# Prompt attention of an MLA decoder step: probabilities transposed on VectorE in 32-by-32 blocks, values taken in 32-row tiles

## What is computed

```python
N_HEADS, QK_NOPE, QK_ROPE, V_HEAD, KV_LORA, SEQ = 16, 64, 32, 64, 256, 1024
def mla_attend_prompt(q_nope, q_rope, c_kv, k_r, w_a_uk, w_a_uv):
    k_nope = jnp.einsum('bsc,chd->bshd', c_kv, w_a_uk)
    v = jnp.einsum('bsc,chd->bshd', c_kv, w_a_uv)
    def block(args):                      # 128 queries at a time
        qn_b, qr_b, i = args
        sc = (jnp.einsum('bqhd,bkhd->bhqk', qn_b, k_nope)
              + jnp.einsum('bqhd,bkd->bhqk', qr_b, k_r)).astype(jnp.float32) * ATTN_SCALE
        sc = jnp.where(k_pos[None, :] <= q_pos[:, None], sc, -jnp.inf)
        p = jax.nn.softmax(sc, axis=-1).astype(v.dtype)
        return jnp.einsum('bhqk,bkhd->bqhd', p, v)
```

## Time and profile before

| | |
|---|---|
| median of 3 runs | 1532.52 us (1532.19 to 1536.1) |
| the profiled execution's own time | 1532.18 us |
| its span, first to last instruction | 1530.5 us |
| PE busy (share of the span) | 1505.8 us (98%) |
| PE weight loads | 1372.2 us (90%) |
| DVE, ACT, POOL busy | 934.7, 551.6, 243.8 us |
| granted PE clock | 0.999 of full |
| DMA | 117.73 MB, mean 77 GB/s |

### The profile page before, as it was taken

The page is one execution under the profiler, slowest core; times in us unless marked ns, Lnnn a source line. Parts: engine busy times, 40 slices in busy tenths (PEclk is TensorE's granted clock), DMA queues, the critical chain, the costliest instruction groups (busy, mean ns, idle before and its releaser), DMA issues.

```text
span 1530.5 us, 32080 instructions
## 1 busy us (share of the span) xinstructions
PE 1505.8 (98%) x11757; PEld 1372.2 (90%) x11757; DVE 934.7 (61%) x1722; ACT 551.6 (36%) x1187; POOL 243.8 (16%) x431
## 2 busy tenths in 40 slices
PE   8999999999999999999999999999999999999998
PEld 7988888888887677778899999999999999999996
DVE  5675667666667788367664645554544545554557
ACT  5465665556664223232331312212131312112146
POOL 2010011101115541000030211212020311112000
PEclk9999999999999999999999999999999999999999
DMA  7112121111133998351220202022020202021003
GB/s 231 51 40 56 38 41 30 39 38 37 23 105 93 301 309 274 112 169 42 81 86 28 69 14 69 15 67 68 20 62 27 69 14 69 14 69 55 1 28 125
DMA packets 158655, 117.73 MB, mean 77 GB/s; under 512 B 55263, under 2 KB 145821, under 8 KB 158416
## 3 DMA queue, kind: packets, MB, share of 16 engines
q1 hardware_dynamic: 143280, 94.40, 20.9%
q10 hardware_dynamic: 11664, 11.44, 2.3%
q0 software_dynamic: 3600, 10.43, 2.1%
HBM read 106.08 MB, written 14.34 MB: 79 GB/s over the span
## 4 chain that ended last, share of the span: by engine, by line
PE 49%; DVE 1%; issue 0%; ACT 0%; DVEq 0%
PE banks L2120 16%; PE banks L2121 16%; PE banks L2122 16%; PE banks L2203 0%; PE banks L2205 0%; PE banks L2204 0%; PE banks L2190 0%; DVEq L1939 0%; DVE weight_stage L2523 0%; DVE down_stage L2523 0%; DVE weight_stage L2536 0%; DVE down_stage L2536 0%; DVE f_stats L2495 0%; ACT up_hi L2345 0%; ACT up_hi L2341 0%
## 5 line engine op out<-in xcount | busy, mean ns | idle before, releaser
L2120 PE MATMUL banks<-act_hi,up_hi 128*128 128x352 f32 (+2 forms) x1040 | 335.5, 323 | 0.8 <-PEq L1691 0.8
L2122 PE MATMUL banks<-act_hi,up_lo 128*128 128x352 f32 (+2 forms) x1040 | 335.4, 323 | 0.0
L2121 PE MATMUL banks<-act_lo,up_hi 128*128 128x352 f32 (+2 forms) x1040 | 335.1, 322 | 0.0
L2120 PEld LDWEIGHTS banks<-act_hi,up_hi 128*128 128x128 f32 x1040 | 195.3, 188 | 1.0 <-issue 1.0
L2121 PEld LDWEIGHTS banks<-act_lo,up_hi 128*128 128x128 f32 x1040 | 195.5, 188 | 0.0
L2122 PEld LDWEIGHTS banks<-act_hi,up_lo 128*128 128x128 f32 x1040 | 195.4, 188 | 0.0
L2423 DVE TENSOR_TENSOR o_t<-o_t,banks 128x352 f32<-128x352 f32 x240 | 121.0, 520 | 95.1 <-PE banks L2122 94.9
L2402 DVE SCALAR_TENSOR_TENSOR conv_out<-conv_in,conv_now,conv_out 128x1072 f32<-128x1072 f32 x42 | 64.7, 1540 | 185.2 <-ACT conv_out L2276 185.2
L1118 DVE TENSOR_REDUCE neg_max<-banks 128x1 f32<-128x896 f32 (+7 forms) x128 | 96.6, 755 | 105.5 <-PE banks L880 104.6
L2267 ACT ACTIVATE conv_in<-banks 128x352 f32<-128x352 f32 x84 | 36.4, 459 | 336.4 <-PE banks L2122 336.4
L2120 PE MATMUL banks<-gated_hi,down_hi 128*128 128x352 f32 x480 | 155.9, 325 | 0.0
(11 more groups left out here) (342 smaller groups left out, 3066.7 us busy)
## 6 DMA issues: line engine op xcount, KB each, us to landing
weight_stage<-in_w_f_up SPq DMA_DIRECT2D x44, 512.0 KB, 4.6
page_slot<-in_cache_kv_latent SPq DMA_DIRECT2D x100, 128.0 KB, 3.7
down_stage<-in_w_f_down SPq DMA_DIRECT2D x22, 512.0 KB, 4.3
page_slot<-in_cache_kv_latent ACTq DMA_DIRECT2D x51, 128.0 KB, 3.8
rope_rows<-in_cache_k_rope SPq DMA_DIRECT2D x256, 16.0 KB, 2.0
rope_slot<-rope_rows SPq DMA_DIRECT2D x16, 256.0 KB, 4.1
z<-in_x_prompt SPq DMA_DIRECT2D x8, 512.0 KB, 3.4
o_blocks<-o_t POOLq DMA_DIRECT2D x30, 128.0 KB, 2.2
```

The source lines that it names most:

```text
L2120: nc.tensor.matmul(o, ws[0], xs[0], start=first, stop=False)
L2121: nc.tensor.matmul(o, ws[0], xs[1], start=False, stop=False)
L2122: return nc.tensor.matmul(o, ws[1], xs[0], start=False, stop=last)
```

## The change

- The probabilities are transposed by DVE in 32-by-32 blocks, SBUF to SBUF, one instruction a unit (`probs_t`); PE's transposes and the copies out of banks 4 and 5 on ACT and DVE go.
- After such a transpose, partitions 32i to 32i+31 hold the keys of a 32-key block for the queries 32i to 32i+31 of the tile. So V must be in all four groups of 32 partitions. DVE transposes it blockwise out of PSUM (`v_t`), SP stores it in DRAM (`store_v`, four DMAs of 1024 pieces of 32 numbers) and loads it back four times per head (`load_v`).
- `values` runs once per head, when its eight units are done: for each of 32 blocks of 32 keys, for each of two sides (four query tiles each), for each of the four groups one matmul with a 32-row, 64-column stationary and 32 to 128 moving columns; side c writes partitions 64c and up, group i writes bank 4+i. That is 240 matmuls per head.
- The units go head by head, query tiles 7, 0, 6, 1, 5, 2, 4, 3.
- The sums of a head stay in one tile; DVE takes one reciprocal per head, and PE makes rows of them with eight small products, the inverse sums broadcast to 64 columns as stationary and the identity as moving operand (`inverse_rows`). The product with the inverse sums is one DVE instruction of 512 columns per head.
- The low halves of q and of the next pair's weights move from DVE to POOL (`q_low`, `split_first`, `split_second`). k's high and low halves are made head by head.
- All stores of the output move from POOL to SP, two DMAs per head. The rope copies are issued by fours (one register load instruction for four pages), 40 per pair in pairs 0 to 5. The first page loads of `decode` move from the first pair to the end.
- `values` of a pair's second head runs in the next pair's step 2, that of the first head in step 10.

```diff
-OWN_AT = {0: "t0", 2: "t1", 3: "ql"}
-NEXT_AT = {4: "wt", 5: "v0", 6: "v1", 8: "k1", 9: "q02", 10: "q12", 11: "q01", 12: "q11", 14: "k0", 15: "q00", 16: "q10"}
-INV_AT = {7: 3, 10: 2, 13: 1}
-SPLIT_AT = {2: "q", 3: "v", 6: "k"}
-VALUES_AT = {5: (3, 0, 2), 7: (3, 2, 4), 9: (2, 0, 2), 11: (2, 2, 4), 14: (1, 0, 4)}
-OUT_AT = {9: 3, 13: 2, 16: 1}
+UNITS = [(hh, t) for hh in range(2) for t in (7, 0, 6, 1, 5, 2, 4, 3)]
+OWN_AT = {0: ["q12", "q11"], 3: ["ql"], 4: ["q10"]}
+NEXT_AT = {5: ["wt"], 6: ["q02"], 7: ["q01"], 8: ["q00"], 11: ["k1"], 12: ["k0"], 13: ["v0"], 14: ["v1"]}
+INV_AT = {1: 1, 9: 0}
+VALUES_AT = {2: 1, 10: 0}
+OUT_AT = {3: 1, 11: 0}
+SIDES = [(0, 2, 5, 7), (6, 4, 3, 1)]
+FIRST_BLOCK, STRIDE = [72, 0], [24, 28]
...
         @block.sync
+            def store_v(p):
+                sp.wait_ge(pj_dve, dve_count(p, "v1"))
+                for a in range(4):
+                    sp.dma_start(m.v_rows[p % 2, a // 2, :, :, 32 * (a % 2):32 * (a % 2) + 32],
+                                 vq[32 * a:32 * a + 32, :, :].rearrange("k a (j d) -> k (a j) d", d=32)).then_inc(v_out, 16)
+            def load_v(p, hh):
+                for i in range(4):
+                    sp.dma_start(v_blocks(p, hh)[32 * i:32 * i + 32, :], m.v_rows[p % 2, hh].rearrange("k j d -> k (j d)")).then_inc(v_in[hh], 16)
+            for p in range(PAIRS - 1):
+                if p:
+                    sp.wait_ge(pv, head(p - 1, 1))
+                    load_v(p, 1)
+                    store_o(p - 1, 1)
+                gather(10 * p + 1, 10 * p + 4)
+                if p + 2 < PAIRS:
+                    sp.wait_ge(w.lo_ok, w.lo_count(p + 1, "q1"))
+                    sp.wait_ge(pj, pj_count(p + 1, "wt"))
+                    w.load(sp, io, p + 2)
+                gather(10 * p + 4, 10 * p + 8)
+                store_o(p, 0)
+                gather(10 * p + 8, 10 * p + 11)
+                store_v(p + 1)
+                v_stored(sp, p + 1)
+                if p + 2 < PAIRS:
+                    load_v(p + 1, 0)
...
         @block.gpsimd
+            for p in range(PAIRS - 1):
+                pool.wait_ge(pj, pj_count(p, "v1"))
+                w.split_first(nc, pool, p + 1)
                 if p:
+                    q_low(p, "q12")
+                    q_low(p, "q11")
+                    q_low(p, "q10")
+                    pool.wait_ge(pj, pj_count(p, "q10"))
+                w.split_second(nc, pool, p + 1)
+                for name in ("q02", "q01", "q00"):
+                    q_low(p + 1, name)
...
         @block.tensor
-            def transposes(p, n):
...
+            def values(p, hh):
+                pe.wait_ge(xt_ok, p * NU + 8 * hh + 8)
+                pe.wait_ge(v_in[hh], (WD_IN if hh == 0 else 0) + 64 * (p + 1))
...
+                for j in range(4 * TT - 4):
+                    for c in range(2):
+                        if slots_at(c, j) is None:
+                            continue
+                        a, b = slots_at(c, j)
+                        blocks = slice(block_of(c, a, j), block_of(c, b - 1, j) + 1, STRIDE[c])
+                        for i in range(4):
+                            r = slice(32 * i, 32 * i + 32)
+                            last = nc.tensor.matmul(ps[64 * c:64 * c + 64, 4 + i, 32 * a:32 * b], v[r, j, :], x[r, hh, blocks, :],
+                                                    start=j == 0, stop=j == last_block(c))
                 last.then_inc(pv, 1)
+            def inverse_rows(p, hh):
...
+                for slot in range(4):
+                    for c in range(2):
+                        last = nc.tensor.matmul(ps[64 * c:64 * c + 64, bank, slot * P:(slot + 1) * P],
+                                                   rinv[:, hh, slot, c:c + 1].to_broadcast([P, V_HEAD]), m.ident[:, :], start=True, stop=True)
...
         @block.vector
+            def v_t(p, name):
+                dve.wait_ge(pj, pj_count(p, name))
+                if p:
+                    dve.wait_ge(v_out, WD_IN + 64 * p)
+                nc.vector.transpose(vq[:, int(name[1]), :], ps[:, proj_bank(p, name), :]).then_inc(pj_dve, 1)
+            def probs_t(p, n):
+                hh, t = UNITS[n]
+                c, slot = side_of(t)
                 dve.wait_ge(pr, p * NU + n + 1)
+                if n % 8 == 0 and p:
+                    dve.wait_ge(pv, head(p - 1, hh))
+                a, wd = block_of(c, slot, 0), (t + 1) * P
+                out = x[:, hh, a:a + wd // 32, :].rearrange("p j c -> p (j c)")
+                nc.vector.transpose(out, prob[n % 2][:, 0:wd]).then_inc(xt_ok, 1)
```

More of the change, by code:

```diff
@@ L578, in load, with swap, split_hi @@
                          [:, :, p * P:(p + 1) * P]).then_inc(self.staged, 16)
[L580 to L588, removed]
+    def swap(self, nc, hh):
+        half, q, rope = ROPE // 2, self.q_staged, (NOPE, 0)[hh]
+        for at, to in ((rope + half, rope + ROPE), (rope, rope + ROPE + half)):
+            last = nc.gpsimd.tensor_copy(q[:, :, hh, to:to + half], q[:, :, hh, at:at + half])
+        return last
+    def split_hi(self, nc, pool):
+        pool.wait_ge(self.staged, self.LOADS)
+        q = self.q_staged
+        self.swap(nc, 0)
+        self.swap(nc, 1).then_inc(self.swapped, 1)
+        pool.wait_ge(self.swapped, 1)
         nc.gpsimd.tensor_copy(self.q_halves[0][:, :, :, :], q[:, :, :, :])
@@ new lines, in load_v, with gather @@
+            def load_v(p, hh):
+                for i in range(4):
+                    sp.dma_start(v_blocks(p, hh)[32 * i:32 * i + 32, :], m.v_rows[p % 2, hh].rearrange("k j d -> k (j d)")).then_inc(v_in[hh], 16)
+            def gather(first, end):
+                for at in range(4 * first, min(4 * end, DEC_BATCH * N_PAGES), 4):
+                    f, b = at // 8, at % 8 // 4
+                    pages = nc.values_load_multi_w_load_instructions(m.pages[0:1, at:at + 4], [sp.engine])[1]
+                    for j, page in enumerate(pages):
+                        sp.dma_start(m.rope_rows[f // 2, :, f % 2, b, j, :],
+                                     io["cache_k_rope"][bass.ds(page, 1)].rearrange("o p c -> (o p) c")).then_inc(gathered, 16)
@@ L747, in _ @@
             sp_pages(nc, io, m, sp, 4)
+            sp.wait_ge(pv, head(PAIRS - 1, 0))
+            load_v(PAIRS - 1, 1)
             sp_pages(nc, io, m, sp, 5)
-            for g in (1, 0):
-                sp.wait_ge(of_ok, seq(PAIRS - 1, g) + 1)
-                o_out(sp, PAIRS - 1, g).then_inc(m.o_last, 16)
+            store_o(PAIRS - 1, 0)
+            store_o(PAIRS - 1, 1)
         @block.gpsimd
@@ L792, in _ @@
             queries(nc, m, 0)
-            for g in (3, 2):
-                store_o(PAIRS - 1, g)
+            pool.wait_ge(pv, head(PAIRS - 1, 0))
+            pool_pages(nc, io, m, pool, 5)
         @block.tensor
@@ L895, in values @@
-            def values(p, g, first, end):
-                at = tp_before(NU - 4 * g)
-                pe.wait_ge(pt_act, p * HALF_TPU + (at + 1) // 2)
-                pe.wait_ge(pt_dve, p * HALF_TPU + at // 2)
-                if first == 0:
-                    pe.wait_ge(pj_act, act_count(p, "t1"))
-                    if seq(p, g):
-                        pe.wait_ge(of_ok, seq(p, g))
-                n = 2 * g + 2
-                for j in range(n * first // 4, n * end // 4):
-                    q = slice(P if j == 2 * g + 1 else 0, 2 * P)
-                    for hh in range(2):
-                        d = slice(hh * V_HEAD, (hh + 1) * V_HEAD)
-                        last = nc.tensor.matmul(ps[d, 6, q], v[:, j, d], pt[:, g % 2, hh, j, q], start=j == 0, stop=j == 2 * g + 1)
-                if end < 4:
-                    return
-                last.then_inc(pv, 1)
@@ L1451, in _ @@
             k = 0
+            for i in range(2):
+                pool.wait_ge(m.o_st[i], 32 * PAIRS)
             for q in range(1, DPAIRS):
```

593 lines of the change are left out of this document (293 added, 300 removed).

## The result

| | before | after |
|---|---|---|
| median of 4 runs | 1533.5 us (1532.2 to 1536.1) | 1686.5 us (1684.6 to 1689.9) |
| ratio | | 1.0998, 95% interval 1.0973 to 1.1022 |
| span, granted PE clock | 1530.5 us, 0.999 | 1684.0 us, 0.942 |

What follows compares the result with a forecast made beforehand. PE was taken to bound the prompt's attention. Pairs 1 to 6 win 33.6 us, pair 0 and the last 6.2, the end loses 3.5: net 36.3 off 1532.2, so 1496 us, range 1476 to 1556.

Steps and rivals of the forecast that it cites:

- What bounds the kernel now: Prompt's attention: PE, busy 98% of the span, sets the pace, 49.1 us a pair.
- What leaves PE, 19.4 us a pair: PE, per pair: transposes of probabilities, V and inverse rows, the old values and changes back to fp32r products go, 19.4 us.
- the inverse rows: PE, per pair: eight small matmuls per head that make rows of inverse sums come on, 2.2 us.
- the values are the open price: PE's new value products, 240 matmuls a head: between 4.1 and 13.6 us, taken as 5.0 a head, 10.0 a pair.
- the lower end: Value products priced by columns alone, as 144 records of 256 columns: 4.1 us a head.
- 0.5 us for narrow rounds: Value products: in half of the 32 key blocks weight loading outlasts 32 moving columns, 0.5 us a head.
- 10.0 of values, 33.3 - 3.0 of DVE, and 3.2 of semaphores: Length of a pair: values and DVE's work mostly not side by side, plus waits, 43.5 us.
- the sum of PE: PE's work per pair after removals and additions: 49.1 - 19.4 + 2.2 + 10.0 = 41.9 us.
- DVE's sum of 33.3: DVE's work per pair (maxima, transposes, low halves of k, scalings of q and more): 33.3 us, against some 32 before.
- SP, 45.7 us: SP's queue per pair (rope copies, weights, V, stores): 45.7 us, 32 to 53; lag fits the slack, costed at nothing.
- Rival one: Value products cost by the record, 28.3 ns each: 13.6 us a head, 142 us more, 1638 us; chance 0.23.
- Rival three: DVE paces the stage further, 46 us a pair: 7 x 2.5 lost, 1513 us; chance 0.09.

Runs made afterwards that it cites:

- experiment 9: Kernel before, its value products read as bf16 from the upper halves of the fp32 numbers, one record instead of two: 1490.5 us.
- experiment 2: Changed kernel, all 240 matmuls a head, but from the second key block on each multiplies only its last 32 moving columns: 1693.5 us.
- experiment 3: Changed kernel with 14 unread 512-column products added after 60, 120 and 180 value matmuls, in the first seven pairs' rows: 1708.9 us.
- experiment 1: Changed kernel, each head making only the value products of its first 32-key block, 8 matmuls in place of 240: 1506.6 us.
- 12: Changed kernel with values cut to 8 matmuls a head and 12 of 40 rope copies a pair issued by ScalarE instead of SP: 1493.3 us.
- 10: Changed kernel, values read as bf16 upper halves, row cut into two pieces of 120 matmuls, projections behind moved one step on: 1540.9 us.
- 11: Changed kernel, bf16 upper-half values in two pieces of 120 matmuls, 12 of 40 rope copies a pair issued by ScalarE: 1542.4 us.
- 5: Changed kernel, value row cut into three pieces of 80 matmuls with score products between, projections moved one to two steps on: 1684.5 us.
- experiment 7: Changed kernel with V's stores and loads of pairs 1 to 6 cut to single pieces, DMA instructions, waits and order kept: 1672.9 us.
- experiment 4: Changed kernel with 7 unread 512-column products added after 60, 120 and 180 value matmuls, in the first seven pairs' rows: 1656.6 us.

## Why the prediction was wrong, step by step

- **What bounds the kernel now**: right (experiment 9).
- **What leaves PE, 19.4 us a pair, and the inverse rows**: right to 1.1 us. 49.1 - 19.4 + 2.2 = 31.9 was said for all but the values, 33.0 is there.
- **The step that failed: "the values are the open price"**, with "I take the lower end". 5.0 us a head was taken, 13.4 came: 16 x 8.4 = 135 of the 190 us. The lower end rested on columns, which experiment 2 shows to count for nothing in the time of a row here. (Its 0.5 us for narrow rounds also took half of the 32 key blocks; by the kernel's table of sides 12 of them have a side with 32 moving columns, 16 of the 60 rounds.) There are two prices in the 13.4. With no shortage a head costs 6.5 us (experiment 3), 13.5 ns a record: 1.5 over my sum. The other 6.9 are standing still for instructions and the lower clock in the row, to which the sum gave no term. I looked at durations, queues and engines, never at where PE's instructions come from; the DMA kind for them stood on the page of before as well, with 67 packets over 1530 us.
- **The clock**: no term at all. Products outside the rows that run at 1.2 GHz, after PE stood still in the row, cost the pair at 197.06 4.6 us. With the gaps filled this is zero in that pair; with the values cut short it still cost some 2 to 4.5 us a pair, by the same estimate.
- **"10.0 of values, 33.3 - 3.0 of DVE, and 3.2 of semaphores"**: 33.5 was said for what is not values, 40.4 came: 8 x 6.9 = 55, the rest of the miss. PE's waits, 2.8, were about what I gave; the sum of PE was 1.1 short, and the clock makes the rest. DVE's sum of 33.3 was 2.6 too high.
- **SP, 45.7 us**: near (47.2 measured in experiment 1), and costed rightly at nothing while a pair is longer than that. Whether it would have paced a kernel whose values cost 5.0 us is not shown: with the values nearly free it did (experiments 1 and 12), with values of half the records in two pieces it did not (10 and 11).
- **Rival one** had the number, 13.6 us a head, and the wrong mechanism: 28 ns is no price of a record, which goes at 8.8 to 15 ns here when nothing is short. That the number came out right is luck: the blocks' 3.45 to 4.0 us over 128 records happen to be 27 to 31 ns a record. I gave it 0.23, arguing that "with 256 columns there, columns explain those 28.3 ns wholly". That argument was sound and still no ground for the lower end: it only said that rows 6 show nothing of narrow records.
- **Rival three** did not come: DVE is busy 30.7 us a pair, and PE waits for exponentials 12.3 us in the whole stage.
- **The range**: its high end held values of 8.7 us a head, and none of the clock.

By the estimate from experiment 3, with ideal supply the change as it stands would break even: 48.8 us a pair against 49.1.

## What to carry to other kernels

Count instructions, not only columns and durations: on PE an fp32 product that isn't a transpose is four (two records and two weight loads), and in this kernel PE stood still where 256 instructions lasted less than about 3.5 us. A burst is free up to the rest of one block and one more (here 126 to 253 records), so many small products belong between long ones rather than in one row, if what is moved for it does not come too late for its readers (experiments 5, 10, 11). Where PE begins to have idle time, put a term for its lower clock beside it. To see a shortage of instructions in a profile, look for idle time put down to "issue", for bursts of exactly 128 matmul records, and for the packets of the kind "instruction".

## What the runs showed of the hardware that I had not expected

- PE's instructions arrive in blocks of 256, 16 KB each. Each starts only when PE has entered the block before, and PE goes on 1.20 to 1.53 us after it has landed. In rows that use them up blocks begin 3.45 to 4.0 us apart, whatever the products' width (experiments 2, 7); with 120 records and 1.8 us of other work to a block hardly a gap is left (experiment 4).
- Bulk transfers delay them: 4.13 us of gap beside V's load of four times 256 KB, 1.43 without (experiment 7).
- On 32-row, 64-column tiles, eight in turn, a matmul with one record took 8.8 ns, and a record of an fp32 one 10.1 (32 columns) to 15 ns.
- Adding work made the kernel faster: 76 us more of products, 30 us less time, since the work fell where PE stood still; the mean granted clock rose from 0.942 to 0.982.
- Left open: why the clock also falls in the pairs with hardly any values (0.89 to 0.96, experiments 1, 12), where PE's single waits are at most 2.6 us apart from those for V's load.
